# Gated linear attention: head outputs with tokens on partitions, their norm's sums taken by ScalarE

## The reference

```
qe = q * exp(b_cum)                      # b_cum: cumulated log decays in a chunk
a = (qe @ (k * exp(-b_cum)).T) * mask    # inside a chunk
o = a @ v + qe @ s_in                    # s_in: state at the chunk's start
s = decay * s + (k * exp(b_last - b_cum)).T @ v
y = rms_norm(o_f + flip(o_b), g) * silu(r)      # norm over the 128 value channels
```

## Time and profile before

| | |
|---|---|
| median of 3 runs | 2791.74 us (2791.06 to 2796.97) |
| the profiled execution | 2786.2 us, its span 2784.4 us |
| TensorE matmuls busy | 2709.7 us, 97% of the span |
| VectorE, ScalarE, GpSimd busy | 49%, 38%, 41% |
| chain that ended last | TensorE 77%, VectorE 11% |

### The profile page before, as it was taken

One profiled execution on the slowest core, in us unless ns is written; L12 is line 12 of the kernel. 1 busy time (PEld: TensorE's weight loads), 2 busy tenths in 40 slices (PEclk: granted clock), 3 DMA queues, 4 the chain that ended last, 5 costly groups with the idle time before them and its releaser, 6 DMA issues.

```text
span 2784.4 us, 34714 instructions
## 1 busy us (share of the span) xinstructions
PE 2709.7 (97%) x12860; PEld 2208.0 (79%) x12860; DVE 1372.0 (49%) x2216; ACT 1067.2 (38%) x1561; POOL 1141.4 (41%) x490
## 2 busy tenths in 40 slices
PE   6999999999999999999999999999999999999998
PEld 4888887788888888888778888887767778888886
DVE  5333347663232533325765333245764566674645
ACT  2222246452222522224654222255465543442332
POOL 2444444244444444444424444464322324344343
PEclk9999999999999999999999999999999999999999
DMA  7545432145454364543214545343210214323231
GB/s 286 191 169 193 152 136 91 47 161 210 167 202 145 107 225 152 200 164 121 82 55 165 213 152 211 137 149 133 106 46 33 74 54 159 114 91 106 91 106 46
DMA packets 70437, 378.83 MB, mean 136 GB/s; under 512 B 7905, under 2 KB 8673, under 8 KB 39809
## 3 DMA queue, kind: packets, MB, share of 16 engines
q1 hardware_dynamic: 65280, 358.56, 36.0%
q10 hardware_dynamic: 4992, 18.09, 1.8%
HBM read 368.23 MB, written 8.39 MB: 135 GB/s over the span
## 4 chain that ended last, share of the span: by engine, by line
PE 77%; DVE 11%; DVEq 4%; ACT 3%; issue 2%; DMA 1%; ACTq 1%; POOL 1%; SPq 1%; POOLq 0%
PE psum L534 21%; PE psum L536 20%; PE psum L535 20%; PE psum L553 1%; PE psum L555 1%; PE psum L554 1%; DVE psum L1769 1%; PE psum L711 1%; PE psum L713 1%; PE psum L712 1%; PE psum L646 1%; PE psum L644 1%; PE psum L645 1%; DVEq L2205 1%; DVE small L1982 1%
## 5 line engine op out<-in xcount | busy, mean ns | idle before, releaser
L451 POOL TENSOR_TENSOR w_lo<-raw,w_hi 128x1024 fp32r<-128x1024 f32 x464 | 1118.6, 2416 | 1482.1 <-ACT w_hi L1149 1467.2
L1149 ACT CAST w_hi<-raw 128x1024 fp32r<-128x1024 f32 x464 | 484.4, 1049 | 851.9 <-PE psum L536 696.8
L534 PE MATMUL psum<-h_hi,w_hi 128*128 128x512 f32 x1920 | 750.3, 391 | 7.7 <-DVE h_lo L1766 4.6
L535 PE MATMUL psum<-h_lo,w_hi 128*128 128x512 f32 x1920 | 747.7, 389 | 0.0
L536 PE MATMUL psum<-h_hi,w_lo 128*128 128x512 f32 x1920 | 747.7, 389 | 0.0
L534 PEld LDWEIGHTS psum<-h_hi,w_hi 128*128 128x128 f32 x1920 | 360.9, 188 | 86.3 <-issue 6.6
L535 PEld LDWEIGHTS psum<-h_lo,w_hi 128*128 128x128 f32 x1920 | 361.0, 188 | 75.1 <-issue 0.5
L536 PEld LDWEIGHTS psum<-h_hi,w_lo 128*128 128x128 f32 x1920 | 360.8, 188 | 75.3
L1852 DVE TENSOR_TENSOR psum<-act_ring,psum 128x512 f32<-128x512 f32 x85 | 59.2, 696 | 516.1 <-ACT act_ring L1219 515.8
L534 PE MATMUL psum<-hid_hi,w_hi 128*128 128x512 f32 x792 | 308.4, 389 | 0.8 <-DVEq L1801 0.8
L536 PE MATMUL psum<-hid_hi,w_lo 128*128 128x512 f32 x792 | 308.1, 389 | 0.0
(11 more groups left out here) (398 smaller groups left out, 3304.9 us busy)
## 6 DMA issues: line engine op xcount, KB each, us to landing
raw<-in_weights_dram SPq DMA_DIRECT2D x232, 1024.0 KB, 5.1
mod_raw<-in_mod_w_dram SPq DMA_DIRECT2D x192, 512.0 KB, 4.0
first_mods_a<-in_mod_w_dram SPq DMA_DIRECT2D x8, 512.0 KB, 11.4
first_mods_b<-in_mod_w_dram SPq DMA_DIRECT2D x8, 512.0 KB, 15.6
prod<-in_cond_rows_dram ACTq DMA_DIRECT2D x8, 512.0 KB, 3.4
first_mods_a<-gate_spill ACTq DMA_DIRECT2D x4, 1024.0 KB, 10.8
gate_spill<-gate_out_c ACTq DMA_DIRECT2D x5, 512.0 KB, 3.0
x<-in_xT_dram SPq DMA_DIRECT2D x1, 2048.0 KB, 9.0
```

The costliest lines, as they stand in the source:

```text
L451: pool.tensor_tensor(w_lo[:, k % 2, cs], raw[:, k % 4, cs], w_hi[:, k % 2, cs].bitcast(F32), ALU.subtract).then_inc(lo_ready, 1)
L534: pe.matmul(out, wh, rhs_hi[:, c, :], start=(c == ks[0]), stop=False)
L535: pe.matmul(out, wh, rhs_lo[:, c, :], start=False, stop=False)
L1149: act.copy(w_hi[:, k % 2, cs], raw[:, k % 4, cs]).then_inc(hi_ready, 1)
```

## The change

The output of a gated head is formed with tokens on partitions. A chunk's 64 tokens of `qe` are the stationary operand and the state the moving one; even chunks write the partitions 0 to 63, odd ones 64 to 127 of the same 128 columns. These products come first, ahead of the wait for `am`; then `gla_pre`, then the products with `am` as stationary operand. The sum of squares over channels is now along the free axis: four activations of ScalarE with an accumulator each, one for 128 tokens; VectorE makes `var` from them (`gla_var`), GpSimd `rstd` as before, and ScalarE copies the output to SBUF scaled by `rstd`, again in four pieces. TensorE turns the result (4 transposes) behind three quarters of the next filler block, and `gla_out` is one operation. The initial state is read where it lies (`state`), not copied. On ScalarE the wait for `yg_ready` moves from before the first half's cast to behind it, and `gla_turned` from before the second half's cast to behind it. In the last head the second filler block is laid as in the others. `summed` corrects the counts of four semaphores; the same correction stands in `rms_cols`, `x_cols`, `rms_var` and three waits for `rb_ready`, which are left out here.

```diff
@@ -372,6 +373,14 @@
 
             bank, at = (2 * d + c % 2, c // 2) if width == T else (c % 2, 2 * d + c // 2)
             return psum[:, S_BANK + bank, at * P:(at + 1) * P]
+
+        def state(h, d, c):
+
+            return s0[:, 4 * d + h, :] if c == (0 if d == 0 else T // GLA_CHUNK - 1) else states[:, d, c, :]
+
+        def summed(r):
+
+            return r + 1 - (GLA_HEADS if r >= R_X2 else 0)
 
         def first_mod(pos):
             return (first_mods_a, first_mods_b)[pos // 2][:, pos % 2, :, :]
...
@@ -877,7 +886,7 @@
                 turn(psum[:, T_BANK, :], t_ring[:, 0, :], pairs)
                 if u > 4:
 
-                    pe.wait_ge(rows_read, u - 4)
+                    pe.wait_ge(yg_ready, u - 4)
                 turn(psum[:, T_BANK + 1, :], t_ring[:, 1, :], pairs).then_inc(turn_ps, 1)
 
             def gla_updates(u, width):
...
@@ -925,14 +934,11 @@
 
             def beside_norm(k, h):
 
-                last = h == GLA_HEADS - 1
-                quarters(G2, k, (0,) if last else (0, 1), hx)
+                quarters(G2, k, (0, 1, 2), hx)
                 if h >= 0:
-                    rms_cols(R_GLA + h, T, ssq, O_BANK)
-                quarters(G2, k, (1,) if last else (2,), hx)
-                if h >= 0:
-                    rms_rows(R_GLA + h, T, O_BANK - 1)
-                quarters(G2, k, (2, 3) if last else (3,), hx)
+                    pe.wait_ge(og_ready, h + 1)
+                    turn(psum[:, O_BANK, :], o_sb, T // P).then_inc(og_turned, 1)
+                quarters(G2, k, (3,), hx)
 
             def gla_tokens(h):
                 u, pairs = 4 + h, T // P
...
@@ -942,27 +948,26 @@
                 gla_turns(u, gv[:, h % 2, :], T)
                 quarters(G2, FILLERS[u][1], (0,), hx)
                 gla_updates(u, T)
-                last = h == GLA_HEADS - 1
-                quarters(G2, FILLERS[u][1], (1,) if last else (1, 2), hx)
+                quarters(G2, FILLERS[u][1], (1, 2), hx)
                 pe.wait_ge(chain_ready, 2 * u + 1)
                 for d in range(2):
                     for p in range(pairs):
                         mm = pe.matmul(psum[:, S_BANK + d, p * P:(p + 1) * P], kn[:, d, p * P:(p + 1) * P],
                                        qe[:, d, p * P:(p + 1) * P], start=True, stop=True)
                 mm.then_inc(a_ps, 1)
-                quarters(G2, FILLERS[u][1], (2, 3) if last else (3,), hx)
+                quarters(G2, FILLERS[u][1], (3,), hx)
                 pe.wait_ge(chain_ready, 2 * u + 2)
+                out = psum[:, T_BANK, :]
+                for d in range(2):
+                    for c in range(2 * pairs):
+                        r = GLA_CHUNK * (c % 2)
+                        pe.matmul(out[r:r + GLA_CHUNK, c // 2 * P:(c // 2 + 1) * P], qe[:, d, c * GLA_CHUNK:(c + 1) * GLA_CHUNK],
+                                  state(h, d, c), start=(d == 0 and c < 2), stop=False, skip_group_check=True)
                 pe.wait_ge(am_ready, h + 1)
                 if h < GLA_HEADS - 1:
                     gla_pre(u + 1, krope, T)
-                out = psum[:, T_BANK, :]
                 for p in range(pairs):
-                    pe.matmul(out[:, p * P:(p + 1) * P], gvt[:, p, :], am[:, p, :], start=(p == 0), stop=False, skip_group_check=True)
-                for d in range(2):
-                    for c in range(2 * pairs):
-                        cs = slice(c * GLA_CHUNK, (c + 1) * GLA_CHUNK)
-                        mm = pe.matmul(out[:, cs], states[:, d, c, :], qe[:, d, cs], start=False,
-                                       stop=(d == 1), skip_group_check=True)
+                    mm = pe.matmul(out[:, p * P:(p + 1) * P], am[:, p, :], gvt[:, p, :], start=False, stop=True, skip_group_check=True)
                 mm.then_inc(og_ps, 1)
 
             products(G2, CTX_K, ch, waits=(ctx_h_ready, 0), width=TC, between=lambda: x_cols(R_FINAL1, 6))
...
@@ -1394,12 +1399,15 @@
                     hh, j = (k - GLA_K) // 2, (k - GLA_K) % 2
                     s = hh % 2
 
-                    if hh >= 2:
-                        act.wait_ge(yg_ready, hh - 1)
+                    def buffers_free():
+                        if between is not None:
+                            between()
+                        if hh >= 2:
+                            act.wait_ge(yg_ready, hh - 1)
                     if j == 0:
-                        evac(k, [(gk[:, s, :], ACT.Copy), (gq[:, s, :], ACT.Copy)], None, between, behind)
+                        evac(k, [(gk[:, s, :], ACT.Copy), (gq[:, s, :], ACT.Copy)], None, buffers_free)
                     else:
-                        evac(k, [(gv[:, s, :], ACT.Copy), (gr[:, s, :], ACT.Silu)], g_in, between, behind)
+                        evac(k, [(gv[:, s, :], ACT.Copy), (gr[:, s, :], ACT.Silu)], g_in, buffers_free)
 
             def gla_logs(u, width):
 
...
@@ -1445,17 +1453,22 @@
             def gla_tokens(h):
                 u = 4 + h
                 gla_decays(u, T)
-                filler(FILLERS[u][0], None, lambda: gla_turned(u, T))
+                filler(FILLERS[u][0])
+                gla_turned(u, T)
                 filler(FILLERS[u][1])
                 if h < GLA_HEADS - 1:
                     gla_logs(u + 1, T)
                 act.wait_ge(og_ps, h + 1)
-                act.activation(ssq[:, :], psum[:, T_BANK, :], ACT.Square)
-                act.drain().then_inc(ssq_ready, 1)
+                for p in range(T // P):
+                    act.activation(ssq[:, p * P:(p + 1) * P], psum[:, T_BANK, p * P:(p + 1) * P], ACT.Square,
+                                   accum_out=small[:, 0, p:p + 1])
+                act.drain().then_inc(og_sums, 1)
+                act.wait_ge(rstd_ready, R_GLA + h + 1)
                 if h:
-
-                    act.wait_ge(yg_ready, h)
-                act.copy(o_sb[:, :], psum[:, T_BANK, :]).then_inc(og_ready, 1)
+                    act.wait_ge(og_turned, h)
+                for p in range(T // P):
+                    act.activation(o_sb[:, p * P:(p + 1) * P], psum[:, T_BANK, p * P:(p + 1) * P], ACT.Copy, scale=rstd[:, p:p + 1])
+                act.drain().then_inc(og_ready, 1)
 
             def mla_act():
                 def take_keys(p, part):
...
@@ -2117,15 +2130,12 @@
                     dve.wait_ge(u_ps[d if full else 1], u + 1)
                     order = list(range(chunks)) if d == 0 else list(range(chunks))[::-1]
                     last = s0[:, 4 * d + h, :]
-                    if full:
-                        dve.tensor_copy(states[:, d, order[0], :], last)
-                        dve.drain()
                     for i, c in enumerate(order):
                         kv = update(d, c, width)
                         e = c * GLA_CHUNK + (GLA_CHUNK - 1 if d == 0 else 0)
                         if full:
                             if i + 1 < chunks:
-                                dve.scalar_tensor_tensor(states[:, d, order[i + 1], :], states[:, d, c, :], prod[:, d, e:e + 1], kv,
+                                dve.scalar_tensor_tensor(states[:, d, order[i + 1], :], state(h, d, c), prod[:, d, e:e + 1], kv,
                                                          ALU.mult, ALU.add)
                                 dve.drain()
                         elif i == 0:
...
@@ -2158,14 +2168,16 @@
                     rotate_keys()
                 gla_chain(u, TC)
 
+            def gla_var(h):
+
+                dve.wait_ge(og_sums, h + 1)
+                dve.tensor_scalar(var[:, 0:T // P], small[:, 0, 0:T // P], 1.0 / P, EPS, ALU.mult, ALU.add).then_inc(var_ready, 1)
+
             def gla_out(h):
 
-                dve.wait_ge(rb_ready, R_GLA + h + 1)
-                dve.wait_ge(og_ready, h + 1)
-                dve.scalar_tensor_tensor(y_gla[:, h, :], o_sb[:, :], par2[:, C2["gla_norm"]:C2["gla_norm"] + 1],
-                                         psum[:, O_BANK, :], ALU.mult, ALU.mult)
-                dve.drain().then_inc(rows_read, 1)
-                dve.tensor_tensor(y_gla[:, h, :], y_gla[:, h, :], gr[:, h % 2, :], ALU.mult)
+                dve.wait_ge(og_turned, h + 1)
+                dve.scalar_tensor_tensor(y_gla[:, h, :], psum[:, O_BANK, :], par2[:, C2["gla_norm"]:C2["gla_norm"] + 1],
+                                         gr[:, h % 2, :], ALU.mult, ALU.mult)
                 dve.drain().then_inc(yg_ready, 1)
 
             def gla_tokens(h):
...
@@ -2182,19 +2194,17 @@
                 dve.drain()
                 last = h == GLA_HEADS - 1
                 if last:
-
-                    for c in range(4):
+                    for c in range(3):
                         split(om_hi[:, c, :], om_lo[:, c, :], o_mla[:, c, :])
-                    dve.drain()
-                if last:
-                    rms_var(R_GLA + h, T, P, O_BANK)
+                    gla_var(h)
+                    split(om_hi[:, 3, :], om_lo[:, 3, :], o_mla[:, 3, :])
                     for c in range(GLA_HEADS - 1):
```

(2 more changed lines are left out.)

15 lines of the change are left out of this document (8 added, 7 removed).

## The result

| | before | after |
|---|---|---|
| median | 2793.31 us (2791.06 to 2796.97, 4 runs) | 2773.26 us (2771.28 to 2776.41, 4 runs) |
| the profiled execution | 2786.2 us, span 2784.4 us | 2776.41 us, span 2774.6 us |
| TensorE matmuls busy | 2709.7 us, 97% | 2702.7 us, 97% |

The ratio of after to before over all these runs is 0.9932, with a 95% interval of 0.9919 to 0.9946. In the two profiled executions the gap is only 9.8 us.

What follows compares the result with a forecast made beforehand. TensorE's instructions and clock were taken as the bound. The heads' marks gave -10.3 us, two new clock falls +2.5, so -7.8, applied to the median 2791.74: 2783.9 us, range 2778.5 to 2792.

Steps and rivals of the forecast that it cites:

- The states' part: TensorE, each gated head: 32 half-width instructions in 1.75 us instead of 3.52, minus 1.77 a head.
- the rival without pairing: States' part: column halves run one after the other, 3.5 us; 2790.5 us in all; chance 0.08.
- The wait for `og_ready`: TensorE before the turn of `o_sb`: new idle of 3.3 us in three heads, none in the last.
- The -10.3: Stretch of the gated heads: its end moves from 2314.7 to 2304.4, before new clock falls are charged.
- The 1.1 us given to the cast ahead of the turned keys: Last head, ScalarE: the `w_hi` cast now precedes the copies of the turned keys, plus 1.1 us.
- The wait for `am`: TensorE ahead of the decay products: 1.8 us idle in two heads, filled by 1.75 us of states and ended.
- The last head's 2.6 us: TensorE's wait before the last head's scores, gone because the second quarter (2.8 us) moves ahead of them.
- the low end of the range: Whole kernel: 2778.5 us, from terms for cheaper copies (-1.8) and no clock falls (-2.5).
- I apply the difference to the median: Whole kernel: forecast -7.8 us applied to median 2791.74, though the profiled execution was 5.5 below it: 2783.9 us.
- 0 or +5.1 in the range: Range term: whether the timed runs have head 1's long clock fall, which cost 5.1 us of 10.2.
- The rival "slower": Waits for `og_ready`: clock stays down 10.2 us in three heads, +3.8 net or +8.9; 2795.5 to 2800.6; chance 0.09.
- two for +2.5 forecast: Three new waits for `og_ready`: two clock falls, each 1.65 us less 0.4 slack, +2.5; ends none and three.

Runs made afterwards that it cites:

- behind_with_copies: states_behind with the eight copies of the initial states put back on VectorE; 2773.77 us, ratio to before 0.9946.
- states_behind: The changed kernel with the states' part back behind the wait for `am` and the decay products; 2771.41 us, ratio to before 0.9944.
- before_no_copies: The kernel before with only the eight copies of the initial states removed; 2778.07 us, ratio to before 0.9960.
- last_quarter_back: The changed kernel with the last head's scores ahead of the third quarter again; 2772.80 us, ratio to before 0.9943.
- comparison executions: 58 executions of the kernel before, timed in alternation with the experiments' kernels; median 2790.8 us (2781.6 to 2797.6), mean clock 0.9886.
- before_again: The kernel before, unchanged, profiled and timed again; 2789.60 us, ratio to before 1.0001.
- after_again: The changed kernel, unchanged, profiled and timed again; 2772.67 us, ratio to before 0.9946.
- states_ahead_wide: The kernel before with the full-width states' part put ahead of the wait for `am`, copies kept; 2782.11 us, ratio to before 0.9973.

## Why the prediction was wrong

**What was right.** The mechanism on TensorE. The states' part: 1.75 forecast, 1.90 measured, where the rival without pairing said 3.5. The sums' products are gone. No wait for `am`. The wait for `og_ready`: 3.3 us in three heads and none in the last forecast, 3.0, 3.0, 3.0 and none measured. Copies 1.2 against 1.14, the table load on the path.

**The sum was 1.6 us short.** The -10.3 holds the 5.1 of before's long fall and no fall behind the new waits. The profile that fits this is behind_with_copies', with the same waits and no fall in the heads: 142.9 us (36.14, 37.42, 37.42 and 31.90), against before's 154.8 a gain of 11.9. Each head is 0.2 to 0.5 us shorter than forecast (36.4, 37.85, 37.8 and 32.4). The 1.1 us given to the cast ahead of the turned keys in the last head are there, as the wait at L900 in states_behind; in after's profile, where the last head takes 30.8 us, the fall in front of it has hidden them.

**Two reasons inside it were wrong without harm.** The wait for `am` was said to be filled by the states' part and ended by the missing copies as well; states_behind and before_no_copies show that the second alone does it. The last head's 2.6 us were given to the moved quarter; last_quarter_back keeps all but 0.6 of them without it. And the low end of the range is 1.1 us lower than its own terms give: 2783.9 - 1.8 - 2.5 is 2779.6, not 2778.5. The measured 2773.3 lies below both.

**The step that failed is the clock's.** It was wrong at three places, the first two on before's side.

First, "I apply the difference to the median". The profiled execution was 5.5 us below the median that was shown, and this was treated as an offset that both kernels share. By the sum below most of it was what the change takes away. Before's executions differ along their clock, and the profiled one, with a clock of 0.990, was among the better ones: 17 of the 58 comparison executions have 0.990 or more. A fall's worth of 5.1 us was seen in it and called one head out of line, to be won or not (0 or +5.1 in the range); that an average execution has more than one such fall was not among the cases.

Second, the price of a wait ahead of L868. Both were priced at their own 1.8 us, with the one fall that was seen behind one of them, and the section on the clock took the falls behind waits at 1.65 us, from L711. Behind the waits for `am`, with narrow products following, a fall, where it came, lasted 6.8 to 13.7 us in the profiles, up to 6.9 us lost. The rival "slower" had such a long fall, but put it at the new wait, where a full quarter follows and it lasted 3.4 us; it belonged to the old wait.

Third, the new falls: two for +2.5 forecast, three for 0.3 measured, since the time that they cost hides waits behind them (states_behind).

By size. The forecast of -7.8 is -5.2 of work and waits, -5.1 for before's one fall and +2.5 for the new ones. The profiles have -11.5 in the heads: -6.8 of work and waits, -5.1 for the fall, +0.3 for the new ones. The medians of before_again and after_again have -16.9. The 5.4 us between are put down to the further falls of before's average execution: at 2.6 us for 0.001, its mean clock of 0.9886 where the first profile has 0.990 is worth 3.6, and before_again's profile shows two more falls and 4.7 us more in the heads. This part is inferred from the mean clocks and two profiles; no execution at 0.985 was profiled.

**What stays open.** The first comparison gave 20.0 us, the second pair 16.9, whose ratio of 0.9946 is 15 of 2790; before's scatter allows all of them. Why a given wait is followed by a fall in one execution and not in the next was not settled; the waits are there each time. Nor was it settled why a fall came in states_ahead_wide with no wait ahead of it.

## What to carry to other kernels

When a kernel's profiled execution is faster than its median, ask what differs between its executions before carrying the difference over: here it was the clock, and each run's mean clock told it. Price a wait of TensorE by what follows it: behind the waits for `am`, with narrow matmuls following, the clock fell for 6.8 to 13.7 us here, behind those with a turn and a full quarter following for 3.4. Add up a forecast and the measurement over the same falls, or the clock is counted twice. A small copy within SBUF on VectorE costs what GpSimd's instruction beside it still has to run, so take it away or move it past that instruction.

## What was not expected of the hardware

- Eight copies of 128x128 cost 11.7 us of 2790: most waited for GpSimd (227 ns alone, 1450 ns on average, up to 2458), this made `am` late by 1.8 us in two heads, and by the mean clocks the falls behind that wait cost more than the wait (7.5 against 3.6 us).
- A fall of the clock can be nearly free: three of 3.4 us each behind the waits for `o_sb` lengthened the stretch of the heads from 142.9 to 143.2 us, since later waits shrank by as much.
- The fp32 products of 64 stationary columns over all 128 rows: 32 instructions in 1.90 us where the two partition halves alternate, 2.50 us where neighbours share one, 3.52 us as full-width stationary operand with 64 moving columns. The rule of the Trainium skill that the prediction weighed (TensorE: Matmul & The Clock Gate, Part 3) has no overlap in either of the first two orders; the runs show a step of 0.6 us between them.
- Three waits of 2.9 to 3.0 us with a turn and a full quarter behind them: falls of 3.4 us behind all three in the profiles of after and after_again, behind one in states_behind's, behind none in behind_with_copies'. Waits of 1.8 us with 6.5 us of narrow products behind: 6.8 to 13.7 us where the fall came, and in some heads none. And once a fall of 3.4 us inside 7.5 us of narrow products with no wait ahead of it (states_ahead_wide).
